# A decoder step on one core: the cache pages of the sample attention loaded as keys of both groups, then values, with one transpose for both groups' keys

## The reference, cut to what matters

```python
# selected blocks: 2048 past tokens in 16 pages of 128 rows, pages found by page_table
past = pool[phys[..., None], rows, g_ix[..., None]]     # cache_kv_slc (N_PHYS, 128, G=2, 2, HD=64)
s = jnp.einsum('bqghd,bqgkd->bqghk', q, k) * (HD ** -0.5)
p = masked_softmax(s, mask)                              # only 16 blocks of 64 rows take part
o = jnp.einsum('bqghk,bqgkd->bqghd', p, v)
# window: the last 512 rows, cache_kv_win (8, 512, G, 2, HD), the same sum without a selection
# memory: 256 tokens, cache_kv_mem (8, 256, 4, 2, 128)
```

## Time and profile before

| what | value |
|---|---|
| median of 3 runs | 2985.07 us (2983.78 to 2989.9) |
| the profiled execution | 2985.64 us |
| its span, first to last instruction | 2984.1 us |
| mean granted clock of PE | 0.915 of 2.4 GHz |
| the stage of the change | 1396 to 1640 us of the span: PE busy 196.4, DVE 124.4, ACT 66.9, POOL 34.4 us; DMA share 0.38 |
| sa_pages DMAs | 64 on SP, 64 on POOL, 128 KB each |

### The profile page before, as it was taken

How to read it: one execution, slowest core, us unless ns; L and a number is a source line. 1 busy time by engine, 2 the same in 40 slices (tenths; PEclk the granted TensorE clock), 3 DMA queues, 4 the chain that set the end, 5 groups by cost and what they waited for, 6 DMA issues and landing times. The chain is left out here.

```text
span 2984.1 us, 40911 instructions
## 1 busy us (share of the span) xinstructions
PE 2582.3 (87%) x15701; PEld 2256.4 (76%) x15701; DVE 1245.8 (42%) x2360; ACT 833.5 (28%) x1831; POOL 156.4 (5%) x221
## 2 busy tenths in 40 slices
PE   5977788798366689995887999998979999999999
PEld 5956588798355567774443999997769989999997
DVE  4156466202533676663554322323143333333334
ACT  3153154433332344441332321212121111111110
POOL 1003221000300000001110000000000000000000
PEclk8988599899686799996897999999989999999999
DMA  4001432301101000003431221123021111111111
GB/s 118 22 11 33 122 108 59 125 30 63 61 1 30 1 1 1 1 1 99 135 122 56 53 54 43 43 53 124 1 57 57 43 43 54 46 43 43 43 43 57
DMA packets 168806, 156.73 MB, mean 53 GB/s; under 512 B 18802, under 2 KB 149781, under 8 KB 168564
## 3 DMA queue, kind: packets, MB, share of 16 engines
q1 hardware_dynamic: 159060, 135.16, 15.0%
q0 software_dynamic: 7072, 18.98, 2.2%
q10 hardware_dynamic: 2496, 0.11, 0.1%
HBM read 142.76 MB, written 15.59 MB: 53 GB/s over the span
## 5 line engine op out<-in xcount | busy, mean ns | idle before, releaser
L177 PE MATMUL ps<-brT_r,ff_wih 128*128 128x344 f32 x1056 | 338.3, 320 | 11.2 <-DVE ff_wi_r L165 11.2
L179 PE MATMUL ps<-brT_r,ff_wi_r 128*128 128x344 f32 x1056 | 337.9, 320 | 0.0
L178 PE MATMUL ps<-xnT_r,ff_wih 128*128 128x344 f32 x1056 | 337.8, 320 | 0.0
L177 PEld LDWEIGHTS ps<-brT_r,ff_wih 128*128 128x128 f32 x1056 | 199.6, 189 | 12.6 <-DVE ff_wi_r L165 11.3
L179 PEld LDWEIGHTS ps<-brT_r,ff_wi_r 128*128 128x128 f32 x1056 | 199.2, 189 | 0.0
L178 PEld LDWEIGHTS ps<-xnT_r,ff_wih 128*128 128x128 f32 x1056 | 198.9, 188 | 0.4
L3194 ACT ACTIVATE ff_sa<-ps 128x344 f32<-128x344 f32 x66 | 30.2, 458 | 589.7 <-PE ps L179 589.7
L177 PE MATMUL ps<-x_r,mg_wh 128*128 128x344 f32 x576 | 184.8, 321 | 11.1 <-DVE mg_w_r L165 11.1
L3223 DVE TENSOR_TENSOR x<-x,ps 128x512 f32<-128x512 f32 (+1 forms) x198 | 135.8, 686 | 129.9 <-PE ps L179 128.6
L178 PE MATMUL ps<-xnT_r,mg_wh 128*128 128x344 f32 x576 | 184.3, 320 | 0.0
L179 PE MATMUL ps<-x_r,mg_w_r 128*128 128x344 f32 x576 | 184.3, 320 | 0.0
(11 more groups left out here) (528 smaller groups left out, 5817.1 us busy)
## 6 DMA issues: line engine op xcount, KB each, us to landing
ff_wi<-in_w_ffn_in SPq DMA_DIRECT2D x44, 512.0 KB, 5.2
mg_w<-in_w_in SPq DMA_DIRECT2D x24, 512.0 KB, 4.0
ff_wo<-in_w_ffn_out SPq DMA_DIRECT2D x11, 1024.0 KB, 4.8
sa_pages<-in_cache_kv_slc POOLq DMA_DIRECT2D x64, 128.0 KB, 2.5
sa_pages<-in_cache_kv_slc SPq DMA_DIRECT2D x64, 128.0 KB, 2.3
sc_X<-in_cache_kv_cmp SPq DMA_DIRECT2D x56, 128.0 KB, 2.2
sc_X<-in_cache_kv_cmp POOLq DMA_DIRECT2D x56, 128.0 KB, 2.4
x<-in_w_in SPq DMA_DIRECT2D x6, 1024.0 KB, 5.3
```

What stands on the lines that cost most here:

```text
L177: nc.tensor.matmul(out, wh, xh, start=(first and k == 0), stop=False)
L178: nc.tensor.matmul(out, wh, xl, start=False, stop=False)
L179: ins = nc.tensor.matmul(out, wl, xh, start=False, stop=(last and k == n - 1))
```

## The change

A page is loaded by two DMAs instead of one: keys of both groups into the first 128 columns of the page's 256, values of both groups into the other 128. Each run is now 256 B long. The window is loaded by four DMAs, one for each of key or value and group. One transpose of 128 columns then turns the keys of both groups of a token tile, so that a fill holds 512 tokens, and its bank is copied whole. There are 1 fill for win, 2 for mem and 4 for slc, 7 for a sample. The semaphore counts of the loads follow, scores() waits for win and slc fill by fill, and attend() reads the values as one run of 128 columns. The loads of the other stages that use `load_pages` keep their form.

```diff
@@ -2085,12 +2085,17 @@
                 dve.wait_ge(kept, 1)
 
 
-def load_pages(eng, cache, dst, pt, b, half, done):
+def load_pages(eng, cache, dst, pt, b, half, done, by_kind=False):
 
     with eng.Fori(0, NPG // 2) as n:
         page = eng.value_load(pt[0:1, bass.ds(n * 2 + (half + NPG * b), 1)], min_val=0, max_val=NPHYS - 1)
-        eng.dma_start(dst[:, bass.ds(n * 512 + half * 256, 256)],
-                      cache[bass.ds(page, 1)].rearrange("o r g c d -> r (o g c d)")).then_inc(done, 16)
+        if by_kind:
+            for cc in range(2):
+                eng.dma_start(dst[:, bass.ds(n * 512 + (half * 256 + cc * G * HD), G * HD)].rearrange("p (g d) -> p g d", g=G),
+                              cache[bass.ds(page, 1), :, :, cc].rearrange("o r g d -> r (o g) d")).then_inc(done, 16)
+        else:
+            eng.dma_start(dst[:, bass.ds(n * 512 + half * 256, 256)],
+                          cache[bass.ds(page, 1)].rearrange("o r g c d -> r (o g c d)")).then_inc(done, 16)
 
 
 def stage_s_compress(M):
@@ -2473,7 +2478,7 @@
         A[k] for k in ("pt", "qz", "qmz", "knT", "gT", "oacc", "selneg", "vrow"))
     units = [(k, b) for b in range(B) for k in ("win", "mem", "slc")]
     NU = len(units)
-    fills_of = {"win": 2, "mem": 2, "slc": 8}
+    fills_of = {"win": 1, "mem": 2, "slc": 4}
     chunks_of = {"win": 1, "mem": 1, "slc": 4}
     fill0, chunk0 = [0], [0]
     for k, _ in units:
@@ -2509,10 +2514,10 @@
         def wait_rows(pe, u):
             k, b = units[u]
             if k == "slc":
-                pe.wait_ge(in_s[b % 2], 8 * NPG * (b // 2 + 1))
-                pe.wait_ge(in_p[b % 2], 8 * NPG * (b // 2 + 1))
+                pe.wait_ge(in_s[b % 2], 16 * NPG * (b // 2 + 1))
+                pe.wait_ge(in_p[b % 2], 16 * NPG * (b // 2 + 1))
             else:
-                pe.wait_ge((in_win if k == "win" else in_mem)[b % 2], 16 * (b // 2 + 1))
+                pe.wait_ge((in_win if k == "win" else in_mem)[b % 2], (64 if k == "win" else 16) * (b // 2 + 1))
 
         bank = lambda f: ps[:, (0, 1, 2, 7)[f % 4], :]
 
@@ -2529,18 +2534,11 @@
             eng.wait_ge(turned, f + 1)
             if u >= 2:
                 eng.wait_ge(scored, chunk0[u - 1])
-            if k == "mem":
-                parts = [(kTb[u % 2][:, j * 512:(j + 1) * 512], bank(f))]
+            dst = kTb[u % 2][:, j * 512:(j + 1) * 512]
+            if f % 2 == 0:
+                nc.scalar.activation(dst, bank(f), ACT.Copy).then_inc(kept_a, 1)
             else:
-
-                parts = [(kTb[u % 2][g * HD:(g + 1) * HD, j * 256:(j + 1) * 256],
-                          bank(f)[0:HD, g * 256:(g + 1) * 256]) for g in range(G)]
-            for dst, src in parts:
-                if f % 2 == 0:
-                    ins = nc.scalar.activation(dst, src, ACT.Copy)
-                else:
-                    ins = nc.vector.tensor_copy(dst, src)
-            ins.then_inc(kept_a if f % 2 == 0 else kept_v, 1)
+                nc.vector.tensor_copy(dst, bank(f)).then_inc(kept_v, 1)
 
         def wait_fills(eng, n):
             if (n + 1) // 2:
@@ -2554,9 +2552,12 @@
                 for b in range(B):
                     if b >= 2:
                         sp.wait_ge(attended, 3 * (b - 2) + 1)
-                    sp.dma_start(rows[b % 2][:, 0, 0:4 * 256].rearrange("p (t n) -> p t n", t=4),
-                                 I["cache_kv_win"][b].rearrange("(t p) g c d -> p t (g c d)", p=P)
-                                 ).then_inc(in_win[b % 2], 16)
+                    for cc in range(2):
+                        for g in range(G):
+                            sp.dma_start(rows[b % 2][:, 0, 0:4 * 256].rearrange(
+                                             "p (t c g d) -> p t c g d", t=4, c=2, g=G)[:, :, cc, g],
+                                         I["cache_kv_win"][b][:, g, cc].rearrange("(t p) d -> p t d", p=P)
+                                         ).then_inc(in_win[b % 2], 16)
                     if b >= 2:
                         sp.wait_ge(attended, 3 * (b - 2) + 2)
                     sp.dma_start(rows[b % 2][:, 1, :].rearrange("p (t n) -> p t n", t=2),
@@ -2564,14 +2565,14 @@
                                  ).then_inc(in_mem[b % 2], 16)
                     if b >= 2:
                         sp.wait_ge(attended, 3 * (b - 2) + 3)
-                    load_pages(sp, I["cache_kv_slc"], pages[:, b % 2, :], pt, b, 0, in_s[b % 2])
+                    load_pages(sp, I["cache_kv_slc"], pages[:, b % 2, :], pt, b, 0, in_s[b % 2], by_kind=True)
 
             @block.gpsimd
             def _(pool):
                 for b in range(B):
                     if b >= 2:
                         pool.wait_ge(attended, 3 * (b - 2) + 3)
-                    load_pages(pool, I["cache_kv_slc"], pages[:, b % 2, :], pt, b, 1, in_p[b % 2])
+                    load_pages(pool, I["cache_kv_slc"], pages[:, b % 2, :], pt, b, 1, in_p[b % 2], by_kind=True)
 
             @block.tensor
             def _(pe):
@@ -2586,19 +2587,16 @@
                         if f >= 4:
                             wait_fills(pe, f - 3)
                         for a in range(4):
-                            if k == "mem":
-                                src, m = kv[:, j * 1024 + a * 256:j * 1024 + a * 256 + XD], P
-                            else:
-                                o = (2 * j + a % 2) * 256 + (a // 2) * 128
-                                src, m = kv[:, o:o + HD], HD
-                            ins = nc.tensor.transpose(bank(f)[0:m, a * P:(a + 1) * P], src, c("ident"))
+
+                            o = j * 1024 + a * 256
+                            ins = nc.tensor.transpose(bank(f)[:, a * P:(a + 1) * P], kv[:, o:o + P], c("ident"))
                         ins.then_inc(turned, 1)
 
                 def scores(u):
                     k, b = units[u]
-                    wait_fills(pe, fill0[u + 1])
                     for j in range(chunks_of[k]):
                         n = chunk0[u] + j
+                        wait_fills(pe, fill0[u + 1] if k == "mem" else fill0[u] + j + 1)
                         if n >= 2:
                             pe.wait_ge(skept, n - 1)
                         out = ps[0:heads(k), 3 + n % 2, :]
@@ -2640,7 +2638,7 @@
                             rhs = kv[:, t * 1024:(t + 1) * 1024].rearrange("p (h c d) -> p h c d", c=2, d=XD)[:, :, 1, :]
                             out = ps[0:nh, 6, 0:512]
                         else:
-                            rhs = kv[:, t * 256:(t + 1) * 256].rearrange("p (g c d) -> p g c d", c=2, d=HD)[:, :, 1, :]
+                            rhs = kv[:, t * 256 + P:(t + 1) * 256]
                             out = ps[0:nh, 6, 0:P]
                         ins = nc.tensor.matmul(out, w, rhs, start=(t == 0), stop=(t == full - 1 and k == "mem"))
                     if k != "mem":
```

## The result

| | before | after |
|---|---|---|
| median | 2985.61 us (4 runs, 2983.78 to 2989.9) | 3018.79 us (4 runs, 3016.51 to 3023.5) |
| ratio to before | 1 | 1.0111 (95%: 1.0094 to 1.0129) |
| profiled execution, its span | 2985.64, 2984.1 | 3016.51, 3014.9 |
| stage: SP's first window load to its first load of mg_w | 1395.54 to 1640.02, 244.5 | 1394.47 to 1671.05, 276.6 |
| PE, DVE, ACT, POOL busy in it | 196.8, 124.4, 66.9, 34.4 | 183.2, 104.8, 48.8, 92.1 |

What follows compares the result with a forecast made beforehand. The prediction took a ring of page loads and PE, lengthened by POOL's DMA issue, as the bound. Stalls +32.9, turns -8.1 and start +0.1 gave +25 us on 2985.64: 3010 us, range 2994 to 3060.

Steps and rivals of the forecast that it cites:

- six stalls: PE's waits from attend(slc b-2) to turn(slc b), b = 2 to 7: 22.1 us each, 132.5 against 99.6, +32.9.
- six turns, low clock behind them counted: Slc turns of samples 2 to 7: 30.3 us falls to 6 x 3.7 = 22.2, with 0.3 each for slower following work.
- start, to the end of attend(slc 0): Pages of sample 0 come 5.6 us later, cheaper turns save 2.8 and 2.7: +0.1; sample 1's pages cost 0.
- after the end of attend(slc 6): Stage's end: after the last turn nothing changes, 0.
- The ring: Attention of the samples: page loads wait for PE and PE for loads; one turn grows from 27.8 to some 32 us.
- SP stays ahead of POOL, so this costs nothing by itself: SP's page loads: second DMA adds 0.46 us a page, making 14.5 us a sample, still ahead of POOL.
- the 4.2: Time from POOL's last page issue to the start of turn(slc b), taken as 4.2 us again after the change.
- POOL's term: POOL's page loads: a second DMA adds 0.70 us a page, so first to last issue becomes 16.45 us, 5.6 more.
- Rival A: Page loads: packets bind; 256 B ones cost near 48.9 ns, 8.6 us more in each of seven loads, 3070; chance 0.20.
- Rival B: POOL's page loads: second DMA runs in the 1.01 us idle gap between page DMAs, so faster, 2973 us; chance 0.08.
- Rival C: Page loads: second DMA costs 0.54 us and landing 2.6, so 2990 us, read as no change; chance 0.07.

Runs made afterwards that it cites:

- e5: The changed kernel, still two DMAs a page, but each a plain 512 B run per partition, one per group; window in one DMA: 3016.51 us, ratio 1.0102.
- e6: The changed kernel with one DMA a page, cut into the same 512 runs of 256 B, four pieces in a partition: 2974.15 us, ratio 0.9955.
- e9: The kernel before, with SP's window and memory loads of a sample held until the previous sample's page turn has begun: 2972.37 us, ratio 0.9951.
- e10: e5 with window and memory loads of a sample held until the previous sample's page turn has begun: 3002.78 us, ratio 1.0053 to before.
- e4: The changed kernel, but POOL's pages come by one DMA each as before, SP's stay at two: 3021.89 us, ratio 1.0106.
- e3: The changed kernel, but SP's pages come by one DMA each as before, POOL's stay at two: 3010.30 us, ratio 1.0065.
- e11: The changed kernel reordered on PE: scores(mem), then the previous sample's attend(slc), then turn(slc): 2963.71 us, ratio 0.9923 to before.
- e7: The kernel before with one step moved: the previous sample's attend(slc) stands ahead of turn(slc) on PE: 2988.22 us, ratio 1.0005.
- e1: The change's transposes and copies with the loads of before, one DMA a page and one for the window: 2974.44 us, ratio 0.9950.
- e12: The kernel before reordered on PE: scores(mem), then the previous sample's attend(slc), then turn(slc): 2972.92 us, ratio 0.9951.

## Why the prediction was right

**Result.** 3018.8 lies in the range of 2994 to 3060, slower as forecast (0.85). Sizes, term by term, of the profiled execution:

| term | forecast | measured |
|---|---|---|
| six stalls | +32.9 | +31.7 |
| six turns, low clock behind them counted | -8.1 | -8.7 + 2.2 = -6.5 |
| start, to the end of attend(slc 0) | +0.1 | +8.5 |
| after the end of attend(slc 6) | 0 | -1.6 |
| rest of the kernel | 0 | -1.3 |
| sum | +25 | +30.8 |

The median moved by 33.2 us and the span of the profiled execution by 30.8.

**The ring** was right, as the pitch of 31.8 us against "some 32" shows, and so was its sum of 22.1 for a stall against 21.9. But that the sum came out so near is luck: two errors cancel. The prediction's step "On SP it is 0.35 + 0.11 = 0.46 a page ... SP stays ahead of POOL, so this costs nothing by itself" **failed**: SP's page grew by 1.01, because a second DMA costs a pass 0.56 and not 0.46 (e5) and because a row in pieces adds 0.23 to each DMA (e6), which no term had. So SP's queue ends last, after 0.97 + 18.89 us, where the forecast had POOL's 1.43 + 16.45. Against that, window and memory of the next sample now stand behind SP's own last page, no longer over POOL's: the turn follows the start of SP's last DMA by 2.2 to 2.8 us, not by 4.2. e9 and e10 show that these two loads are what made the 4.2. For one of the landings that the prediction lists they are not the cause: in sample 7 of before, its 3.4, no such load follows, and SP issues last there, 2.1 us before the turn. POOL's term was near: 0.70 taken, 0.64 measured for a second DMA, and e4 shows that it isn't on the path. e3, with SP relieved, is the case that the prediction described, POOL last with those loads beside its last pages, and its stalls are 21.9 as well.

**The start** is where 8.4 us were missed, and by the same step. Pages of samples 0 and 1 stand behind each other on SP, 19.2 and 19.8 us with 23.0 from start to start, so turn(slc 0) waits 12.32 us and turn(slc 1), which "0" was put down for, 3.25 more. e3, which relieves SP alone, has a stage 9.5 us shorter than after (267.1 against 276.6) with stalls no shorter, and 8.7 of the 9.5 lie before the end of attend(slc 0).

**The turns** were near: 16 transposes of 128 columns take 1.97 us in e11 at the full clock, 0.123 each, and 3.6 at the low one against 3.4 forecast. What the low clock costs behind a turn was taken at 0.3 a sample and is 0.4 on average (2.2 in six): scores(mem) takes 2.81 and 3.08 us in two samples of after, 1.89 to 2.10 in the others. One reading was wrong: the 4.53 us of the earlier trace rows for 32 transposes of 64 columns are not at the full clock. The granted clock there is 0.80, and in e7, at 1.00, 32 of them take 3.68, 0.115 each:

```profile
1434.73:1439.20 4.47, 4.47 (x34) 3.99 (x34) 4.16 (x8) 2.60 (x7) 0.00 (x0) 0.80 0.68 233
```

```profile
1525.46:1529.10 3.64, 3.64 (x34) 3.44 (x34) 2.43 (x6) 2.62 (x7) 1.08 (x2) 1.00 0.27 78
```

So a turn saves 1.7 us at the full clock, where the prediction put 2.2. e1 puts the whole benefit at 15 us, but only 4.0 us of it lie in the ring, half of the 8.1 forecast there, since stalls and the work behind the turns grew. The start gives twice as much, 8.0.

**Rival A**, packets bind, falls: 17.1 ns, near the 20 taken, and e6, with packets cut as in after, has e1's time. The Trainium skill ("DMA: Bandwidth & Descriptors", Specifications) states that a transfer runs at line rate from 512 B on and is read, changed and written below that. From it the prediction drew that a 256 B packet costs no less than the 30.9 ns of a 512 B one; on these loads it takes 17.1 ns, and the measurement decides. **Rival B**, a second DMA that hides in POOL's gap, falls by POOL's pitch of 2.19 in e5 and after. Half of its mechanism is real: in e6 the gap does absorb the 0.21 us by which a DMA in pieces is longer, but no second DMA. **Rival C**, level, fell with it.

**Not tried:** a load in cache order with one transpose that picks both groups' keys by a strided operand, or transposes of 64 columns that land in the upper partitions. Either would keep one DMA a page and still save copies. Also not tried were holding back the window and memory loads in after or e11, and holding back only one of the two.

## What to carry to other kernels

Before you save instructions on an engine that waits, look at who loads for it: here half of the transposes were bought with a second DMA a page, and the queues that issue DMAs were the bound, not the bytes and not the packets (8.0 us of the DMA engines' time in 18.9 us of issue). Price a DMA per issue and by shape on each queue, and check every queue, since the one that has slack now needn't keep it. When loads and compute wait for each other in a ring, try an order that frees the buffer sooner. On the kernel before, the first such order (e7) gained nothing and the second (e12) 15 us, as much as the cheaper turns alone (e1); with the dear loads it was worth far more, since the second order turned this change from 33 us of loss into 9 of gain.

## What the hardware showed that was not expected

- **Shape sets the issue cost.** A page DMA with one run in every partition takes 0.35 us on SP and 0.54 on POOL, at 512 B (e5) and at 1 KB. In pieces it takes 0.58 and 0.72 with two pieces (after), 0.585 and 0.749 with four (e6): from one piece to two there is a step, from two to four hardly any. A second DMA in the loop adds 0.56 us to SP's pass and 0.64 to POOL's, more than its own row; what fills the rest the profile doesn't show.
- **Packets of 256 B are cheap:** 17.1 ns on SP's queue, against 30.9 for 512 B and 48.9 for the mostly 1 KB ones of before. For the same bytes that is 11% more than at 512 B.
- **Large loads delay small ones of another queue:** with 1.5 MB issued ahead of them, the last pages land after 5.1 to 6.0 us and not 2.1 to 2.3 (e5 against e10), though the mean DMA share of the stage is only 0.41 in after (0.38 before).
- **A short wait can cost PE nearly as much again behind it:** after 2.03 us of idle time, with 2.13 more shortly before, 32 products take 5.32 us in place of 3.66 (e7). The granted clock there is 0.68 on average, partly at the 1.2 and partly at the 2.4 GHz level; behind the stall of 8 us it is 0.51, as the stretch of after showed. The wait of 2.13 us for the probabilities, which every sample has, is followed by work at a granted clock of 1.00 ahead of turn(slc 4) of before and of 0.56 ahead of turn(slc 3); what decides it is open.
